# One operand of the expert dot products moves from SBUF to two PSUM banks, and later stages use the banks that are left

## The reference, cut to what matters

```python
def block(x, c, ...):
    h = rms_norm(x, norm1_w) * (1 + sc1) + sh1
    z = h @ w_in                                  # q k v u post pre g_attn g_conv
    o_attn = attend(q, k, v, sinks)               # window 128, 16 heads, 4 key/value heads
    o_conv = gate_post * short_conv(gate_pre * u)
    merged = sigmoid(g_attn) * o_attn + sigmoid(g_conv) * o_conv
    x = x + g1 * (merged @ w_out)
    h2 = rms_norm(x, norm2_w) * (1 + sc2) + sh2
    return x + g2 * peer_ffn(h2)

def peer_ffn(h2):                                 # per token t
    s = einsum('thcd,hcnd->thcn', h2 @ w_query, sub_keys)
    idx, g = top16_of_256(top16(s))               # 8 heads x 16 experts
    a = gelu(einsum('thkd,td->thk', expert_u[idx], h2))
    return einsum('thk,thkd->td', g * a, expert_v[idx])
```

## Time and profile before

| | before |
|---|---|
| median of 3 runs | 3754.29 us (3752.93 to 3760.50) |
| the profiled execution | 3759.58 us |
| its span from first to last instruction | 3757.6 us (2.0 us lie around it) |
| PE, DVE, POOL, ACT busy | 85%, 68%, 64%, 29% of the span |
| bytes moved | 1301.41 MB, 346 GB/s over the span |
| first and last dot | 280.0 us and 3715.6 us |

### The profile page before, as it was taken

One profiled execution on the slowest core, in us unless ns is written; L12 is line 12 of the kernel. 1 busy time (PEld: TensorE's weight loads), 2 busy tenths in 40 slices (PEclk: granted clock), 3 DMA queues, 4 the chain that ended last, 5 costly groups with the idle time before them and its releaser, 6 DMA issues.

```text
span 3757.6 us, 34490 instructions
## 1 busy us (share of the span) xinstructions
PE 3176.5 (85%) x9919; PEld 1650.4 (44%) x9919; DVE 2540.2 (68%) x5981; ACT 1103.4 (29%) x2416; POOL 2396.3 (64%) x2146
## 2 busy tenths in 40 slices
PE   8989999498988979998898996877876788788777
PEld 2446777153535435555555652423432334334221
DVE  1338878477777657877777874667766767776663
ACT  1533343142433243332223431223212322322120
POOL 1002434467777757677777675777777777777775
PEclk9999999799999989999999998999999999999999
DMA  8757887989999999999999999999999999999997
GB/s 314 267 204 235 296 266 256 350 319 362 340 381 363 370 340 395 377 391 377 376 393 384 365 362 400 355 362 357 372 365 351 345 378 371 359 370 358 363 365 302
DMA packets 490248, 1301.41 MB, mean 346 GB/s; under 512 B 41880, under 2 KB 177904, under 8 KB 489135
## 3 DMA queue, kind: packets, MB, share of 16 engines
q0 software_dynamic: 304128, 1107.43, 78.7%
q1 hardware_dynamic: 158666, 175.19, 13.8%
q10 hardware_dynamic: 27268, 16.60, 1.4%
HBM read 1277.54 MB, written 23.56 MB: 346 GB/s over the span
## 4 chain that ended last, share of the span: by engine, by line
PE 32%; DMA 23%; POOL 22%; DVE 10%; issue 10%; ACT 2%; SPq 1%; DVEq 0%; ACTq 0%; POOLq 0%
PE bank L1917 16%; DMA v_ring<-in_expert_v_dram,idx 15%; POOL u_ring L734 12%; POOL v_ring L752 11%; PE bank L1941 6%; DMA u_ring<-in_expert_u_dram,idx 6%; DVE u_ring L1478 3%; PE bank L1766 2%; PE bank L1875 2%; PE bank L1857 2%; PE bank L1725 2%; DVE rt L1385 1%; PE bank L1788 1%; DMA ayg<-yg_d 1%; PE bank L1814 1%
## 5 line engine op out<-in xcount | busy, mean ns | idle before, releaser
L1917 PE MATMUL bank<-v_ring,diag 128*128 128x512 f32 (+1 forms) x4032 | 2004.2, 624 | 495.5 <-DMA v_ring<-in_expert_v_dram,idx 397.7
L1478 DVE CUSTOM_DVE_ANT_0 u_ring<-u_ring,h2b 128x1024 f32<-128x1024 f32 x1056 | 1288.0, 1226 | 769.7 <-DMA u_ring<-in_expert_u_dram,idx 715.1
L734 POOL DMA_INDIRECT u_ring<-in_expert_u_dram,idx x1056 | 1198.1, 1135 | 718.7 <-issue 294.6
L752 POOL DMA_INDIRECT v_ring<-in_expert_v_dram,idx x1040 | 1168.0, 1123 | 607.4 <-PE bank L1917 298.2
L1917 PEld LDWEIGHTS bank<-v_ring,diag 128*128 128x128 f32 (+1 forms) x4032 | 721.1, 193 | 1468.7 <-DMA v_ring<-in_expert_v_dram,idx 808.8
L981 ACT ACTIVATE diag<-ident,wgt 128x128 f32<-128x128 f32 x992 | 347.0, 394 | 530.7 <-PE bank L1917 226.5
L1941 PE MATMUL bank<-hi,whi 128*128 128x512 f32 (+1 forms) x832 | 406.9, 489 | 7.9 <-DVEq L1518 4.2
L1941 PE MATMUL bank<-lo,whi 128*128 128x512 f32 (+1 forms) x832 | 309.8, 372 | 0.0
L1941 PE MATMUL bank<-hi,wlo 128*128 128x512 f32 (+1 forms) x832 | 309.7, 372 | 0.0
L973 ACT ACTIVATE act_dot<-dot 128x16 f32<-128x16 f32 x66 | 14.2, 216 | 640.1 <-DVE dot L1478 639.9
L1941 PEld LDWEIGHTS bank<-hi,whi 128*128 128x128 f32 x832 | 158.4, 190 | 80.9 <-issue 65.0
(11 more groups left out here) (281 smaller groups left out, 2623.0 us busy)
## 6 DMA issues: line engine op xcount, KB each, us to landing
wc<-in_w_in_dram SPq DMA_DIRECT2D x104, 512.0 KB, 8.0
wu<-in_w_in_dram SPq DMA_DIRECT2D x26, 1024.0 KB, 9.2
ada_e<-in_w_ada_dram SPq DMA_DIRECT2D x12, 2048.0 KB, 9.9
u_ring<-in_expert_u_dram,idx POOLq DMA_INDIRECT x1056, 6.5
v_ring<-in_expert_v_dram,idx POOLq DMA_INDIRECT x1040, 6.5
wo_sb<-in_w_out_dram SPq DMA_DIRECT2D x2, 4096.0 KB, 25.3
wq_sb<-in_w_query_dram SPq DMA_DIRECT2D x2, 4096.0 KB, 40.2
ayg<-yg_d SPq DMA_DIRECT2D x7, 1024.0 KB, 9.1
```

The costliest lines, as they stand in the source:

```text
L734: pool.indirect_dma_start(out=u_ring[k % RING][:, :], out_offset=None, in_=eu, in_offset=bass.IndirectOffsetOnAxis(ap=idx[n % IDXS][:, k:k ...
L752: pool.indirect_dma_start(out=v_ring[k % RING][:, :], out_offset=None, in_=ev, in_offset=bass.IndirectOffsetOnAxis(ap=idx[n % IDXS][:, k:k ...
L1478: V.tensor_tensor_reduce(out=u_ring[k % RING][:, :], in0=u_ring[k % RING][:, :], in1=h2b[t % 2][:, :], scale=1.0, scalar=0.0, op0=ALU.mult ...
L1917: last = M(banks(c, 1)[0:parts, :], diag[k % DIAGS][:, 0:parts], v[:, c * 512:(c + 1) * 512], start=first, stop=final)
```

## The change

From tile 3 on, h2 is copied by ACT from `h2b` into PSUM banks 6 and 7 at the tile's start (`keep_h2_in_psum`, one 128 x 1024 copy, six in all), and the dots' second input is read from there. The copy waits until all dots of the tile before are done, and the tile's first dot waits for the copy. What used banks 6 and 7 gets by without them:

- group 2's projection uses banks 2 and 3 in turn instead of 2, 3 and 7, so a block waits for the reader of the block two before it, not three;
- in tiles 5 to 7 scores, transposes and outputs of the attention all lie in bank 5, so that a pair's scores wait for the pair before to be finished (`o_kept`); a pair starts every 9 slots, not 5. Tile 5's attention moves from slot 500 to 380, into the projection; tile 6's starts at 624 (642), tile 7's at 742 (770). Merging and output projection of tiles 6 and 7 and of the samples move by 11, 1 and 10 slots, the samples' attention by 8;
- the samples' attention uses banks 2, 3 and 5; its scaled and masked scores take two DVE instructions a group (1024 and 32 columns) instead of one;
- the transposes of the new convolution state move from bank 5 to 2 and 3, three slots later; PE waits for their copy before tile 5's output projection instead of before tile 6's attention.

No matmul, transposition or DMA is added or taken away.

```diff
-ATTN = (None, 24, 86, 138, 190, 500, 642, 770)
-A_PITCH = (None, 4, 5, 5, 5, 5, 5, 5)
-MERGE = (None, 77, 133, 185, 237, 580, 688, 816)
-D_BASE = (None, 86, 135, 187, 239, 582, 690, 818, 930)
-S_BASE = 854
+ATTN = (None, 24, 86, 138, 190, 380, 624, 742)
+A_PITCH = (None, 4, 5, 5, 5, 9, 9, 9)
+MERGE = (None, 77, 133, 185, 237, 580, 699, 817)
+D_BASE = (None, 86, 135, 187, 239, 582, 701, 819, 940)
+S_BASE = 862
...
+LATE = GROUPS[1][0]
+IN_PSUM = 3
+def pbank(at):
+    return PBANKS[at % 3] if at < NPROJ else PBANKS[at % 2]
+def pT_bank(t):
+    return 6 if t < LATE else 5
...
+            def keep_h2_in_psum(t):
+                w(dots_done, t * PH * TOPK)
+                if t in PARKED or t == NT:
+                    w(h2_in, 16 * parked(t) if t < NT else 16 * (len(PARKED) + 4))
+                else:
+                    w(h2_made, t + 1)
+                if t == IN_PSUM:
+                    w(o_kept, LATE * KC)
+                    w(qry_kept, LATE)
+                link(nc.scalar.copy(banks(6, 2), h2b[t % 2][:, :]))
+                act.sem_inc(h2_in_psum, 1)
...
             for n in range(1, UNITS + 1):
+                if n % PH == 0 and n // PH >= IN_PSUM:
+                    keep_h2_in_psum(n // PH)
                 activate_dots(n - 1)
...
-                if at % (PH * TOPK) == 0 and (t in PARKED or t == NT):
-                    w(h2_in, 16 * parked(t) if t < NT else 16 * (len(PARKED) + 4))
+                if at % (PH * TOPK) == 0 and t >= IN_PSUM:
+                    w(h2_in_psum, t - IN_PSUM + 1)
                 V.tensor_tensor_reduce(out=u_ring[k % RING][:, :], in0=u_ring[k % RING][:, :],
-                                       in1=h2b[t % 2][:, :], scale=1.0, scalar=0.0, op0=ALU.mult,
+                                       in1=h2b[t % 2][:, :] if t < IN_PSUM else banks(6, 2), scale=1.0, scalar=0.0, op0=ALU.mult,
...
             def scores_of(i, q):
...
-                if i > KC:
+                if i >= LATE * KC:
+                    w(o_kept, i)
+                    w(v_placed, i // KC + 1)
+                elif i > KC:
                     w(o_kept, i if i % KC == 0 else i - 1)
...
+                    if j == LATE:
+                        w(new_made, 1)
...
-                            if b >= 3:
-                                free_bank(at - 3)
+                            if b >= (3, 2)[g]:
+                                free_bank(at - (3, 2)[g])
...
-                if s == proj_slot(2 * NPROJ - 1) + 8:
+                if s == proj_slot(2 * NPROJ - 1) + 11:
...
-                        if t == 6:
-                            w(new_made, 1)
```

More of the change, by code:

```diff
@@ L863, in copy_pT @@
                     w(pv_ps, i - ring + 1)
-                link(nc.scalar.copy(pT[:, :, :, :].rearrange("p s e t -> p (s e t)"), banks(6, 1)))
+                link(nc.scalar.copy(pT[:, :, :, :].rearrange("p s e t -> p (s e t)"), banks(pT_bank(i // KC), 1)))
                 act.sem_inc(pT_made, 1)
@@ L1072, in attn_steps @@
                             copy_pT(i, pT2, 1)
-                if s == ATTN[NT - 1] + 47:
+                if s == ATTN[NT - 1] + 83:
                     w(k_ps, 1)
-                    link(nc.scalar.copy(kv_row[:, 0:KVW], banks(6, 1)[:, 0:KVW]))
+                    link(nc.scalar.copy(kv_row[:, 0:KVW], banks(5, 1)[:, 0:KVW]))
                     act.dma_start(new_k_prompt.rearrange("a b w g d -> (a b w) (g d)"), kv_row[:, 0:KVW]).then_inc(kv_stored, 16)
@@ L1081, in sample_steps @@
                     w(s_row_ps, 1)
-                    link(nc.scalar.copy(s_row[0:NS, :], banks(7, 1)[0:NS, :]))
+                    link(nc.scalar.copy(s_row[0:NS, :], banks(5, 1)[0:NS, :]))
                     act.sem_inc(s_row_made, 1)
@@ L1604, in sample_steps @@
                         w(s_score_ps, g + 1)
-                        link(V.scalar_tensor_tensor(out=s_sm[:, :], in0=banks(5, 3)[:, 0:NB * WIN + NS], scalar=SCALE,
-                                                    in1=s_mask[:, :], op0=ALU.mult, op1=ALU.add))
+                        for ps, cols in ((banks(2, 2), slice(0, NB * WIN)), (banks(5, 1)[:, 0:NS], slice(NB * WIN, NB * WIN + NS))):
+                            link.note(V.scalar_tensor_tensor(out=s_sm[:, cols], in0=ps, scalar=SCALE,
+                                                             in1=s_mask[:, cols], op0=ALU.mult, op1=ALU.add))
+                        link.settle()
                         link(V.tensor_reduce(smax[:, 0:1], s_sm[:, :], AX.X, ALU.max))
@@ L1776, in transpose_v @@
                 w(pT_made, t * KC)
+                if t >= LATE:
+                    w(o_kept, t * KC)
                 for c in range(2):
-                    last = TR(banks(6, 1)[:, c * P:c * P + P], aq[:, KC + 2 + c, :], ident[:, :])
+                    last = TR(banks(pT_bank(t), 1)[:, c * P:c * P + P], aq[:, KC + 2 + c, :], ident[:, :])
                 last.then_inc(v_ps, 1)
@@ L1795, in transpose_p @@
                     for e in range(2):
-                        last = TR(banks(6, 1)[:, (2 * s + e) * P:(2 * s + e) * P + P], sm[:, e, s * P:s * P + P], ident[:, :])
+                        last = TR(banks(pT_bank(i // KC), 1)[:, (2 * s + e) * P:(2 * s + e) * P + P], sm[:, e, s * P:s * P + P], ident[:, :])
                 last.then_inc(pT_ps, 1)
@@ L1893, in scores @@
                 for q in range(4):
-                    last = M(banks(5, 2)[:, 2 * PK * q:2 * PK * q + 2 * PK], q2b[t % 2][:, n % PH, :],
+                    last = M(banks(2, 2)[:, 2 * PK * q:2 * PK * q + 2 * PK], q2b[t % 2][:, n % PH, :],
                              keys_bd[:, 4 * (n - NT * PH) + q, :], start=True, stop=True)
@@ L1950, in proj_steps @@
                         M(banks(5, 1)[:, 0:n], ones_bd[:, :], sq2[i % 2][:, 0:n], start=True, stop=True).then_inc(ms_ps, 1)
-                if s == proj_slot(2 * NPROJ - 1) + 8:
+                if s == proj_slot(2 * NPROJ - 1) + 11:
                     w(gated, 2 * KC)
-                    w(o_kept, 6 * KC)
+                    for r in range(3):
+                        free_bank(2 * NPROJ - 1 - r)
                     for k in range(KC):
-                        last = TR(banks(5, 2)[0:2 + NB * 2, k * P:(k + 1) * P], new_t[:, k, :], ident[:, :])
+                        last = TR(banks(2, 2)[0:2 + NB * 2, k * P:(k + 1) * P], new_t[:, k, :], ident[:, :])
                     last.then_inc(new_ps, 1)
@@ L1984, in sample_steps @@
                     for c in range(4):
-                        last = TR(banks(7, 1)[0:NS, c * P:c * P + P], qkv_s[:, KC + c, :], ident[:, :])
+                        last = TR(banks(5, 1)[0:NS, c * P:c * P + P], qkv_s[:, KC + c, :], ident[:, :])
                     last.then_inc(s_row_ps, 1)
@@ L1991, in sample_steps @@
                             w(s_pT_made, 2)
+                        else:
+                            w(qry_kept, NT)
                         for b in range(NB):
-                            last = TR(banks(5, 2)[:, b * P:(b + 1) * P], ck_c[:, b, :], ident[:, :])
+                            last = TR(banks(2, 2)[:, b * P:(b + 1) * P], ck_c[:, b, :], ident[:, :])
                         last.then_inc(s_k_ps, 1)
@@ L2002, in sample_steps @@
                             w(s_kept, g)
-                        for at, n in ((0, 512), (512, 512), (1024, NS)):
-                            last = M(banks(5, 3)[:, at:at + n], qz[:, g, :, :, :].rearrange("p r e t -> p (r e t)"),
+                        for to, at, n in ((2, 0, 512), (3, 512, 512), (5, 1024, NS)):
+                            last = M(banks(to, 1)[:, 0:n], qz[:, g, :, :, :].rearrange("p r e t -> p (r e t)"),
                                      kcT[:, e, at:at + n], start=True, stop=True)
```

41 lines of the change are left out of this document (21 added, 20 removed).

## The result

The changed kernel takes 3636.69 us, the median of four runs (3629.93 to 3648.16), against 3753.61 us of the kernel before in the same series: a ratio of 0.9669, with a 95% interval of 0.9641 to 0.9697. The profiled execution took 3637.22 us, its span 3635.2.

The account below looks back on a forecast made before the run. POOL's gathers, stretched under DVE's dots, were taken to set the rhythm of tiles 5 to 7, with DMA the next floor. Terms 83 + 22 + 5 - 4 = 106 us gave 3648 us for the median, range 3590 to 3725.

Parts of the forecast that it names:

- The rival that the dot does not let go: Gathers under dots: with PSUM as second input the hold may stay, nothing is freed and 3757 us remain; 7%.
- Of 157.6 us 142 go and 16 stay: POOL in tiles 5 to 7: of 157.6 us of gather stretching, 142 us vanish with the dot's input in PSUM.
- 287 of 309: Weights for sharing out the stretching in tiles 5 to 7: dots 287, other instructions 11 and 11; dots taken as nine tenths.
- the 83 forecast: Tiles 5 to 7: 83 us gained, at 2.75 us a step and 1056 us in all.
- 2.63 us a step: Tiles 5 to 7: DMA's floor, 413 MB at 410 GB/s in 1008 us, so at most 131 us of gain.
- an estimate of 0.12 us: Tiles 5 to 7: 0.12 us a step added over DMA's floor, for three resources within a tenth of each other.
- The rival of moved waits: POOL gets ahead, then waits for rings and indices; a third of the gain comes, 3715 us; 17%.
- The rival of full transfers: DMA's share of 0.97 to 0.99 means full; POOL's time turns into queueing, some 3750 us; 6%.
- I take 6 us for tile 3: Tile 3: 6 us gained, of at most 26 us by 410 GB/s, with tile 5's attention moving in.
- 16 of the 52.3 us of stretching: Tile 4: 16 us gained, where POOL's 52.3 us of stretched gathers are all there are.
- minus 4 us: Six copies of h2 to PSUM at tile starts: a loss of 4 us, of at most 8.
- The slower rival: Tiles 5 to 7: the attention's nine-slot chain in one bank holds PE, 48 us for 24 pairs; 3785 us; 7%.

Follow-up runs that it names:

- the first experiment: The changed kernel with the dots of tiles 3 to 8 reading h2 from SBUF again, copies, waits and moved slots kept: 3768.34 us, ratio 1.0020 to the kernel before.

## Why the prediction was right, point by point

**The mechanism held.** A dot with one input in PSUM lets gathers go, and that is the whole of the gain: the input put back in SBUF takes it all away. The rival that the dot does not let go falls with the gathers' 0.948 us: in the timeline of tiles 5 to 7 324 gathers begin under a dot, and none of them is stretched. The exchange of operands shows that the doubt behind this rival, the place of the PSUM operand, was empty. No row of before had the dot itself with PSUM; the nearest one, the product at 3299.56 us, told both its length and its effect on POOL.

**The size of the largest term was a little low.** The step that was off is "Of 157.6 us 142 go and 16 stay": 151.2 us went, and 6.4 stayed above 0.940 us a gather. The prediction's own parts, 287 of 309, are 93% and would have given 146; the rounding to nine tenths took 4 us. For the rest, the sum took gathers to fall at any time, and the timelines of tiles 5 to 7 show that they did not. In the kernel before 313 of 769 gathers took 0.98 us or more. Each of them began under a DVE instruction with both inputs in SBUF and ended 0.79 to 0.83 us after it; 306 began under dots, with 155 us of the stretching, and none under a pick. In the changed kernel 25 gathers are stretched, by 8 us, all under picks, norms and products with both inputs in SBUF.

By POOL's account these 9 us are most of the 11 by which tiles 5 to 7 gained more than the 83 forecast. The sum itself went by another floor, that of the transfers, 2.63 us a step, and added an estimate of 0.12 us; 0.10 came (1044.7 against 1008 us). No run shows whether POOL's further relief is what made that smaller. In size the waits agree: 0.22 us a step between POOL's floor (2.53) and the forecast step (2.75) is 84 us, and 81.7 were found.

**What is late next was named rightly.** DMA at 395 GB/s over the three tiles, against the 410 by which the floor of 2.63 us was worked out; the step is 2.72. Fewer bytes shorten it, less work on PE or earlier indices do not. The waits for indices, which the prediction gave as one of three close resources, did come, but another wait stands right behind them. The rival of moved waits was right in kind, 57 us came back, but not in amount, since it left a third of the gain and nearly two thirds of POOL's relief arrived. (By its own third of 106 us it should have read 3719 us, not 3715.) The rival of full transfers falls: a share of 0.97 to 0.99 was no sign of a full queue, for the rate rose from 361 to 400 GB/s in tile 5 with the share going from 0.97 to 1.01.

**Tiles 3 and 4.** 22 us were forecast and 25.5 came, but shared out otherwise: 6 + 16 against 2.0 + 23.5. In tile 3 the step that was off is "I take 6 us for tile 3", under a bound of 26 us worked out from 410 GB/s: that rate was reached in a stretch of tile 4, and tile 3 stayed at 380. The transfers held it there, as the narrower rows in tiles 3 and 4 show, but 380 is not a fixed limit: in the run with half of PE's work in the expert rows it was 389. Why transfers that go at 400 GB/s in tile 5 go no faster in tile 3 is left open beyond that. In tile 4 I took 16 of the 52.3 us of stretching, for the reload of weights; 23.5 came. The moved attention shifted PE's busy time by 11.6 us (354.1 to 365.7 in tile 3, and 345.9 to 334.1 in tile 4), not by 18.

**The small terms.** The samples gave 3.7 us of the 5. The copies were put at minus 4 us; the timeline at tile 5's start shows what they do:

```profile
2463.04 1.22 DVE L1508 CUSTOM_DVE_ANT_0 u_ring<-u_ring,bank 128x1024 f32<-128x1024 f32 x1 [0.19 <-DVE rden L1362]
...
2464.20 0.94 POOL L749 DMA_INDIRECT u_ring<-in_expert_u_dram,idx  x1 [0.30 <-issue]
...
2464.31 1.02 ACT L996 COPY bank<-h2b 128x1024 f32<-128x1024 f32 x1 [0.45 <-DVE dot L1508]
...
2465.44 0.94 POOL L767 DMA_INDIRECT v_ring<-in_expert_v_dram,idx  x1 [0.31 <-issue]
...
2465.55 1.22 DVE L1508 CUSTOM_DVE_ANT_0 u_ring<-u_ring,bank 128x1024 f32<-128x1024 f32 x1 [0.93 <-ACTq L997]
```

The copy sits between two dots that start 2.51 us apart, less than a mean step, and POOL issues through it with 0.30 us between gathers. DVE's cover had shrunk, as foreseen, but the copy fits into the step; it is next to free here. At the starts of tiles 4, 6, 7 and of the samples the two dots are 2.63 to 2.67 us apart, at tile 3's 4.88. What copies and changed schedule cost together, up to 0.4% by the first experiment, had been put at 4 us for the copies and at nothing for the schedule, and no single part was tried alone. The slower rival, PE held by the attention in one bank, did not come. The line of the scores (1825) shows PE's idle time before them over the whole run:

```profile
  issue: 24.2, 49
  DVEq L1368: 6.6, 6
```

The six waits for `keep_o` are as they were in the earlier trace rows, but they all lie before 1190 us, ahead of the attention of tiles 5 to 7; for those 24 pairs, in one bank and nine slots apart, the trace names no such wait. What grew there is idle time for which it names no releaser: 14.5 us in 35 places, against 1.0 us in 4 before. It may hold the new waits, and it stays under the 20 us that the prediction gave as a sign of this rival.

**The signs that were named.** Gathers at a mean near 0.96 us (0.948), dots at 1.226 (1.221), 390 GB/s (391 to 400), a step of 2.75 (2.72), waits grown to some 90 us (81.7, those for indices among them): these came. Tiles 0 to 2 unchanged: 2.3 us longer in sum.

## What to carry to other kernels

Where gathers are issued on POOL, read their durations as a spread: longer ones (0.98 to 1.99 us here) that all end the same time after a DVE instruction's end (0.79 to 0.83 us here) mean that DVE holds them, and the operands of that instruction say what to move. Moving one input to PSUM can free POOL without a faster instruction anywhere. Then work out the rate at which the transfers would have to run, because the gain can stop there (here 94 of 151 us arrived, and 2 of 48 in the tile whose transfers were already at their rate). When a wait shows up on the new bound, remove it alone before counting on it: the wait for indices gave nothing in these tiles when it went.

## What the runs showed of the hardware that was not expected

- A dot over 128 x 1024 with an input in PSUM took 1.221 us and one with both in SBUF 1.225 us. The Trainium skill ("VectorE: DVE Perf Modes", the section on the TRN2 errata) gives a PSUM source a larger fixed cost, by its figures an estimate of 0.065 us a dot; the trace does not show it, and the measurement decides.
- ACT's copy of 128 x 1024 from SBUF into PSUM took 1.017 us, the one out of PSUM 1.008.
- The DMA share is no measure of room: 0.97 at 361 GB/s in the first experiment, 1.01 at 400, 0.92 at 317.
- With about a third fewer matmuls on PE its granted clock in tiles 4 to 7 fell from 0.96 to 0.99 down to 0.72 to 0.84, and the single run took no longer (3633.63 us).
- In tiles 5 to 7 of the kernel before, 20 gathers that began in the last 0.16 us of a dot took no longer than the undisturbed ones; every stretched one began with 0.17 us or more of the instruction to go. Eight that began within 0.03 us of a dot's start were not stretched either; there the dot was the longer one, 1.25 to 1.29 us.
